# A fourth fixed expert in the MoE stage, and the routing tables moved into the output buffers

## The chip, the cores and the metric

One core of one Trainium2 chip runs the whole program in one launch. The metric is the device time of one execution in microseconds. Three runs of the kernel before took 2047.45, 2049.58 and 2053.73 us; their median is 2049.58 us.

## The reference, cut to what matters

The program is two layers of a decoder trunk on 1024 tokens of 1024 fp32 values. Layer 0 mixes with attention and state-space heads, layer 1 with a Conformer convolution. After each mixer comes the same hierarchical mixture of experts (MoE): 4 groups of 8 experts, the best group is chosen for a token, then the best 2 experts in that group, so that 2048 (token, expert) pairs fall on 32 experts in whatever way the router decides. Nothing may be dropped.

```python
g_sel = jnp.argmax(g_logits, axis=-1)
g_w = jnp.take_along_axis(jax.nn.softmax(g_logits, axis=-1), g_sel[:, None], axis=-1)[:, 0]
e_logits = jnp.take_along_axis(e_all, g_sel[:, None, None], axis=1)[:, 0]
top_v, top_i = lax.top_k(e_logits, 2)
gate = (g_w[:, None] * jax.nn.softmax(top_v, axis=-1)).reshape(-1)
eid = (g_sel[:, None] * 8 + top_i).reshape(-1)
...
gu = xb @ w_gate_up[e]                                  # 1024 x 1024 weights of expert e
y = (silu(gu[:, :512]) * gu[:, 512:]) @ w_down[e]       # 512 x 1024
...
x = x + sum over the token's two experts of gate * y
```

## The kernel before, in words

The program is one sequence of stages: mixer of layer 0, MoE of layer 0, Conformer of layer 1, MoE of layer 1. `moe(k, layer)` is the function that the change touches; it runs twice.

**Routing.** PE makes the router's logits, DVE picks the choices `M` (two 0/1 masks of 128 x 8 x 32), PE counts them (L1417, L1418), and DVE makes each pair's rank in its expert (`rank`) and, through one-hot matmuls, a table of which token stands at which rank of which expert (`tabT`). From it come `hidx` (the rows to gather for an expert) and `yidx` (where its output rows go).

**Order and capacity.** Experts 0 to FIXED-1 are worked on first, whatever their counts; that allows their weights to be fetched before the counts are known. Each fixed expert has room for 96 tokens, which is three blocks of TB = 32. The other experts are sorted by count (`nth`, then `place`, then `order`): the FULL = 2 largest have room for 128 tokens, the next LARGE = 13 for 96, the rest for 64. `place_of` sets at which place in the sequence each rank of the sort stands, so that long and short experts alternate. There are 84 blocks in all. An expert's tokens beyond its capacity are *overflow*: `count_overflow` and `place_overflow` compute how many extra passes of 128 rows are needed (`n_over`), `index_overflow` says where each overflowing pair stands.

**The stream of weights.** SP issues all weight loads on one queue: 4 MB of gate-up and 2 MB of down per expert. Gate-up has four buffers (the fourth is the residual `x_res`, which has been parked in DRAM by then), down has three. Down buffer 2 holds the routing tables until they are done with. Experts 0 to 2 come in early; the fourth buffer's first load (L1207 waits for `order_ready`) and the third down load (behind `over_ready`) come when the sort and the overflow tables are finished. From there on the load of expert q waits for PE to be through with the buffer's last user.

**One block.** PE multiplies 32 tokens by gate-up (64 matmuls, L1458), ACT takes silu of one half (L1285), DVE the product (L1627) and a transpose (L1631), PE multiplies by down (32 matmuls, L1473) one block later, ACT copies the result to one of YB = 6 output buffers (L1279, `y_evacuate`), and POOL scatters it to `y_rows` in DRAM by an indirect DMA (L1346). POOL also gathers the rows of an expert by an indirect DMA (L1339), PE turns them (L1440), DVE evacuates them (`xT_evacuate`, L1620).

**Behind the last block.** Each engine reads `n_over` and enters its loop `over` only where that is above 0 (`turns_over`). In such a pass POOL first scatters the overflow table to DRAM (`table`: 16 indirect DMAs), SP waits for them all, then loads 128 slot numbers, the 4 MB and 2 MB of the overflowing expert's weights; POOL gathers the rows, PE turns them and does 64 matmuls of 128 x 128 and 8 of 128 x 512, ACT and DVE the rest, and POOL scatters 128 rows; SP waits for that (`o_stored`). Then, in layer 1, SP loads `y_rows` back (L1250), DVE adds them to `x` (L1712), and SP writes the output.

The output buffers `rows_in_out` hold three gather buffers `xg` (3 x 1024 columns) and six output buffers `y` (6 x 256).

Of the kernel before, what the change touches and what calls it, by code (L numbers as in the profile page):

```python
# [19 lines left out]
AX = mybir.AxisListType  # L20

P = 128
D = 1024
T = 1024
NT = T // P
# [15 lines left out]
NE = NG * EG  # L41
# [7 lines left out]
TB = 32  # L49
FIXED, FULL, LARGE = 3, 2, 13  # L50


XB, YB = 3, 6
TURNS, LAST_FULL = 12, 17
AHEAD = 3
# [977 lines left out]
def moe(k, layer):  # L1033
# [3 lines left out]
    PAD = 1 << 16  # L1037
# [9 lines left out]
    with ExitStack() as ctx:  # L1047
# [18 lines left out]
        def early(shape):  # L1066
            n = math.prod(shape[1:])
            flat = tables[:, used[0]:used[0] + n]
            used[0] += n
            assert used[0] <= KF * D, used  # L1070
            return shaped(flat, shape)

        def part_of(flat, at0, shape):
            return shaped(flat[:, at0:at0 + math.prod(shape[1:])], shape)
# [13 lines left out]
        h = rows_in_out[:, 0:2 * D].rearrange("p (b n) -> p b n", b=2)  # L1088
        y_spare = rows_in_out[:, 4 * D:]
        L = k.logits  # L1090
# [12 lines left out]
        ge, go = sb("ge", [P, NT, NG]), sb("go", [P, NT, NG])  # L1103
        E, W = early([P, NT, NE]), early([P, NT, NE])
        M = early([P, 2, NT, NE])
        M_flat = M[:, :, :, :].rearrange("p j i e -> p (j i) e")
        Msel = early([P, 2, NT, NE])
        in_Msel = Msel[:, :, :, :].rearrange("p j i e -> p (j i e)")
        scan_mask = part_of(in_Msel, 0, [P, NE, NT + 1])
        in_group, met = part_of(in_Msel, 288, [P, NT, EG]), part_of(in_Msel, 352, [P, NT, EG])  # L1110
        rank_sel, fold_sorted = part_of(in_Msel, 416, [P, 2 * NT]), part_of(in_Msel, 432, [P, NE])
        empty, place_col = part_of(in_Msel, 464, [P, NE]), part_of(in_Msel, 496, [P, 1])
        Msel_flat = Msel[:, :, :, :].rearrange("p j i e -> p (j i) e")
        both = early([P, NE, NT + 1])
        top = [sb("top1_", [P, NT]), sb("top2_", [P, NT])]
        ex, den = sb("ex", [P, NT]), sb("m_den", [P, NT])
        pre = early([P, NE, NT + 1])
        rank = early([P, NE, NT])
        key = early([P, NE])
# [12 lines left out]
        order_f = early([P, NE])  # L1132
        cap_e, excess = early([P, NE]), early([P, NE])
        extra, incl, shift, oe = behind[3], behind[4], behind[5], sb("oe", [P, MAX_OVER])
# [18 lines left out]
        fold_ready, chosen, v_ready = sem("fold_ready"), sem("chosen"), sem("m_v_ready")  # L1153
        over_ready, padded, table_made = sem("over_ready"), sem("padded"), k.dma_sems[layer]["table_made"]
        dve_link, pool_link = sem("m_dve_link"), sem("m_pool_link")
# [40 lines left out]
        def _(sp):  # L1196
# [8 lines left out]
            sp.wait_ge(h_ready, NT - SQUARED_EARLY)  # L1205
            sp.wait_ge(x_parked, 16 * (SQUARED_EARLY + 1))
            sp.wait_ge(order_ready, 1)  # L1207
            down = 2
            for q in range(FIXED, NE + 1):
                if q < NE:  # L1210
                    e = sp.value_load(order[0:1, q:q + 1], min_val=0, max_val=NE - 1)
                    if q > FIXED:
                        sp.wait_ge(gu_done, last_of[gu_user[q]] + 1)
                    load_gate_up(sp, e, gu_of[q])
                if q == FIXED:
                    sp.wait_ge(over_ready, 1)
                else:
                    sp.wait_ge(d_done, last_of[q - 4] + 1)
                load_down(sp, down, (q - 1) % 3)
                down = e  # L1220
# [36 lines left out]
        def _(act):  # L1257
# [17 lines left out]
            def y_evacuate(n):  # L1275
                act.wait_ge(d_done, n + 1)
                if n >= YB:
                    act.wait_ge(stored[n % YB], 16 * (n // YB))
                act.activation(y[:, n % YB, :], ps[:, Y + n % 2, 0:D // 4], ACT.Copy).then_inc(y_ready, 1)  # L1279
# [20 lines left out]
        def _(pool):  # L1300
# [37 lines left out]
            def gather(q):  # L1338
                pool.indirect_dma_start(out=xg[:, q % XB, :], out_offset=None, in_=k.hbuf,  # L1339
                                        in_offset=bass.IndirectOffsetOnAxis(ap=hidx[:, q:q + 1], axis=0),  # L1340
                                        bounds_check=last_h, oob_is_err=False).then_inc(gathered[q % XB], 16)
# [18 lines left out]
            for q in range(XB):  # L1360
                gather(q)
            pool.wait_ge(h_index, 2)
            pool.wait_ge(turned, 1)
            pool.wait_ge(gathered[0], 16)
            gather(XB)
            pool.wait_ge(y_index, 1)
            for q in range(NE):
# [140 lines left out]
        def _(dve):  # L1508
# [98 lines left out]
            ts(fold_sorted[:], eid[:], place_col[:, 0:1], None, ALU.is_equal).then_inc(fold_ready, 1)  # L1607
            link(tt(cmp[:], eid[:, :].unsqueeze(2).to_broadcast([P, NE, NE]), place[:, :].unsqueeze(1).to_broadcast([P, NE, NE]), ALU.is_equal))
            dve.wait_ge(spread, 2)
            row_index(ps[:, TOTALS, FIXED:NE], FIXED, NE)  # L1610
            link(tt(cmp[:], cmp[:], eid[:, :].unsqueeze(1).to_broadcast([P, NE, NE]), ALU.mult))
            dve.wait_ge(spread, 3)
# [5 lines left out]
            def xT_evacuate(p, tokens, out):  # L1618
                for half in range(2):
                    tt(xT[:, p, 4 * half:4 * half + 4, 0:tokens], ps[:, TRN + half, :].rearrange("p (k t) -> p k t", k=4)[:, :, 0:tokens],  # L1620
                       g_exp[:, 4 * half:4 * half + 4].unsqueeze(2).to_broadcast([P, 4, tokens]), ALU.mult).then_inc(out, 1)
# [10 lines left out]

            def sort_weights():
                link(dve.tensor_reduce(order_f[:], cmp[:], AX.X, ALU.add))
                dve.tensor_copy(order[:], order_f[:]).then_inc(order_ready, 1)
# [34 lines left out]
            def index_overflow():  # L1670
                link(tt(E[:], rank[:].rearrange("p e i -> p i e"), in_tiles(cap_e[:], NE), ALU.is_lt))
                link(tt(W[:], rank[:].rearrange("p e i -> p i e"), in_tiles(shift[:], NE), ALU.add))
                link(stt(out=W[:], in0=E[:], scalar=float(PAD), in1=W[:], op0=ALU.mult, op1=ALU.add))
                for j in range(2):
                    link(tt(Msel[:, j, :, :], M[:, j, :, :], W[:], ALU.mult))
                link(dve.tensor_reduce(posf[:], Msel_flat, AX.X, ALU.add))
                link(dve.tensor_copy(pos[:], posf[:]))
                dve.sem_inc(over_ready, 1)

            sort_weights()  # L1680
            dve.wait_ge(turned, 1)
            xT_evacuate(0, CAP[0], xT_ready)
            count_overflow()
            place_overflow()
            for n in range(NB):
                q, tl = blocks_of[n]
                hidden(n)
                if tl == 0 and q + 1 < NE:
                    dve.wait_ge(turned, q + 2)
                    xT_evacuate((q + 1) % 2, CAP[q + 1], xT_ready)  # L1690
                if n == 0:
                    index_overflow()
                if n == 3:
                    weigh_choices()
# [606 lines left out]
```

## Time and profile before

| | |
|---|---|
| median of three runs | 2049.58 us |
| the profiled execution | 2048.27 us, span 2046.5 us |
| PE, PE weight loads, DVE, ACT, POOL busy | 91%, 56%, 43%, 21%, 20% of the span |
| mixer of layer 0 with its routing | 0 to 546 us |
| experts of layer 0 | 546 to 1045 us |
| Conformer of layer 1 with its routing | 1045 to 1507 us |
| experts of layer 1 | 1507 to 2005 us |
| sum of the outputs | 2005 to 2046.5 us |

The span runs from the first to the last instruction. The stages were told apart by the lines that run in them. Times in the views are us from the span's start, and a wait is put down to whoever ended it.

### The profile page before, as it was taken

The page shows a single profiled execution, that of the slowest core. Times are in us where ns is not written, and L with a number is a line of the kernel's source. Part 1 is how long each engine was busy: PE and PEld are TensorE (multiplying, and loading weights), DVE is VectorE, ACT ScalarE, POOL GpSimd, SP SyncE. Part 2 cuts the span into 40 slices and gives each one's busy share as a digit, 9 for nine tenths or more (in the row PEclk, how much of TensorE's full clock was granted, in tenths as well). Part 3 has the DMA queues.
Part 4 walks back from the last instruction along what each step waited for, and adds up shares of the span by engine and source line. Part 5 has one row for each costly group of instructions (what it writes and reads, how often), then busy time and mean ns, then how long its engine had stood idle before and what let it go on. Part 6 is the DMA issues. An engine that isn't in the chain of part 4 may idle for free. (4 is left out here: it accounts for less than half of the span.)

```text
span 2046.5 us, 46991 instructions
## 1 busy us (share of the span) xinstructions
PE 1863.8 (91%) x20566; PEld 1148.5 (56%) x20566; DVE 886.1 (43%) x1980; ACT 427.4 (21%) x965; POOL 406.0 (20%) x524
## 2 busy tenths in 40 slices
PE   7999999999699999889969999799879999998892
PEld 5677766666466665656545444345546666655561
DVE  3666666664711111111135999893371121111114
ACT  2433332344011111101023122234401111100110
POOL 2211111012122222222122111120122222222110
PEclk9999999999699999999979999899979999999996
DMA  9200000044699999999887456413589999999996
GB/s 324 80 11 1 11 10 10 0 185 182 259 426 425 427 424 425 426 427 426 369 321 211 86 113 134 108 32 134 217 327 418 425 425 429 425 426 426 425 388 275
DMA packets 94256, 541.95 MB, mean 265 GB/s; under 512 B 23366, under 2 KB 46970, under 8 KB 76392
## 3 DMA queue, kind: packets, MB, share of 16 engines
q1 hardware_dynamic: 68376, 479.13, 57.2%
q0 software_dynamic: 23040, 51.43, 9.0%
q10 hardware_dynamic: 2640, 8.44, 1.0%
q8 instruction: 160, 2.62, 0.5%
q14 instruction: 40, 0.33, 0.1%
HBM read 504.29 MB, written 43.03 MB: 267 GB/s over the span
## 5 line engine op out<-in xcount | busy, mean ns | idle before, releaser
L1627 DVE TENSOR_TENSOR acts<-acts,ps 128x128 f32<-128x128 f32 x168 | 66.3, 395 | 692.0 <-ACT acts L1285 691.6
L1346 POOL DMA_INDIRECT y_rows<-rows_in_out,yidx x168 | 166.6, 992 | 761.5 <-ACT rows_in_out L1279 751.6
L1458 PE MATMUL ps<-wgu,xT 128*32 128x256 f32 x5376 | 306.6, 380 | 0.0
L1473 PE MATMUL ps<-wd,acts 128*32 128x256 f32 x3520 | 215.4, 386 | 26.2 <-issue 23.1
L1458 PEld LDWEIGHTS ps<-wgu,xT 128*32 128x32 f32 x5376 | 176.7, 110 | 109.9 <-issue 5.3
L1285 ACT ACTIVATE acts<-ps 128x128 f32<-128x128 f32 x168 | 46.6, 277 | 632.9 <-PE ps L1458 632.9
L1473 PEld LDWEIGHTS ps<-wd,acts 128*32 128x32 f32 x3520 | 120.1, 111 | 101.9 <-issue 29.9
L1458 PE MATMUL ps<-x_res,xT 128*32 128x256 f32 x2816 | 165.4, 388 | 0.0
L1458 PE MATMUL ps<-early_gu,xT 128*32 128x256 f32 x2560 | 149.7, 387 | 4.1 <-DVE xT L1620 4.1
L2223 DVE SCALAR_TENSOR_TENSOR conv<-dd,par,conv 128x256 f32<-128x256 f32 (+1 forms) x255 | 131.4, 589 | 0.2
L1458 PEld LDWEIGHTS ps<-x_res,xT 128*32 128x32 f32 x2816 | 96.0, 113 | 60.9 <-issue 7.8
L1279 ACT ACTIVATE rows_in_out<-ps 128x256 f32<-128x256 f32 x168 | 64.5, 384 | 292.9 <-PE ps L1473 292.9
L1473 PE MATMUL ps<-early_wd,acts 128*32 128x256 f32 x1856 | 113.5, 385 | 13.1 <-issue 13.1
L864 PEld LDWEIGHTS ps<-m_hT,early_gu 128*128 128x128 f32 x1024 | 116.1, 192 | 4.6 <-issue 3.3
L1458 PEld LDWEIGHTS ps<-early_gu,xT 128*32 128x32 f32 x2560 | 84.0, 112 | 60.5 <-issue 6.7
L864 PE MATMUL ps<-m_hT,early_gu 128*128 128x128 f32 x1024 | 116.9, 275 | 0.7 <-DMA early_gu<-in_w_in 0.7
L1850 PE MATMUL ps<-c_hT,early_wd 128*128 128x512 f32 x256 | 112.7, 593 | 3.4 <-ACT sig L2011 3.2
L1886 PE MATMUL ps<-w_pw,c_hT 128*128 128x512 f32 x256 | 112.4, 593 | 1.5 <-ACT c_hT L2028 1.5
L1858 PE MATMUL ps<-c_hT,early_wd 128*128 128x512 f32 x256 | 112.5, 592 | 0.0
L1620 DVE TENSOR_TENSOR xT<-ps,g_exp 128x384 f32<-128x384 f32 (+2 forms) x128 | 58.9, 502 | 100.2 <-PE ps L1440 100.2
L1473 PEld LDWEIGHTS ps<-early_wd,acts 128*32 128x32 f32 x1856 | 63.1, 111 | 52.8 <-issue 16.7
L918 PE MATMUL ps<-w_out_sb,m_yT 128*128 128x512 f32 x192 | 86.3, 602 | 0.0
(354 smaller groups left out, 2204.5 us busy)
## 6 DMA issues: line engine op xcount, KB each, us to landing
wgu<-in_moe_w_gate_up SPq DMA_DIRECT2D x32, 4096.0 KB, 30.7
wd<-in_moe_w_down SPq DMA_DIRECT2D x42, 2048.0 KB, 29.6
early_gu<-in_moe_w_gate_up SPq DMA_DIRECT2D x18, 4096.0 KB, 29.9
x_res<-in_moe_w_gate_up SPq DMA_DIRECT2D x14, 4096.0 KB, 25.7
early_wd<-in_moe_w_down SPq DMA_DIRECT2D x22, 2048.0 KB, 24.7
early_wd<-in_conv_w_pw SPq DMA_DIRECT2D x22, 512.0 KB, 5.4
conv<-prod POOLq DMA_DIRECT2D x20, 512.0 KB, 4.5
x_res<-x_park SPq DMA_DIRECT2D x2, 4096.0 KB, 31.4
```

Of the source, the lines that this page charges most:

```text
L864: mm = pe.matmul(ps[:, bank, (t % 4) * P:(t % 4 + 1) * P], w_x[:, j, t * P:(t + 1) * P], hT[:, j, :], start=(j == 0), stop=(j == KD - 1))
L918: mm = pe.matmul(ps[:, bank, :], attn_T[p][:, j, :] if j < 4 else yT[:, j, :], w_out[:, j, 512 * half:512 * half + 512], start=(j == 0), s ...
L1279: act.activation(y[:, n % YB, :], ps[:, Y + n % 2, 0:D // 4], ACT.Copy).then_inc(y_ready, 1)
L1346: pool.indirect_dma_start(out=y_quarters, out_offset=bass.IndirectOffsetOnAxis(ap=yidx[:, tl, q:q + 1], axis=0), in_=y[:, n % YB, :], in_o ...
L1458: mm = pe.matmul(ps[TB * g:TB * g + TB, GU + n % 2, 0:2 * P].rearrange("p (a f) -> p a f", a=2), xT[:, q % 2, j, TB * tl:TB * tl + TB], wg ...
L1473: mm = pe.matmul(ps[TB * g:TB * g + TB, Y + n % 2, 0:D // 4], hhT[:, n % 2, TB * j:TB * j + TB], wd[q % 3][:, j, D // 4 * g:D // 4 * g + D ...
L1620: tt(xT[:, p, 4 * half:4 * half + 4, 0:tokens], ps[:, TRN + half, :].rearrange("p (k t) -> p k t", k=4)[:, :, 0:tokens], g_exp[:, 4 * half ...
L1627: tt(hh[:, n % 2, :].rearrange("q (k f) -> q k f", k=KF), by_k(sg[:, n % 2, :]), by_k(ps[:, GU + n % 2, P:2 * P]), ALU.mult).then_inc(hh_r ...
L1850: mm = pe.matmul(ps[:, GATE, :], wg[:, p, j, :], hT[:, j, HALF * h:HALF * h + HALF], start=(j == 0), stop=(j == KD - 1))
L1858: mm = pe.matmul(ps[:, LIN + n % 2, :], wa[:, p, j, :], hT[:, j, HALF * h:HALF * h + HALF], start=(j == 0), stop=(j == KD - 1))
L1886: mm = pe.matmul(ps[:, BACK + half, :], yT[:, j, :], w_pw2[:, j, 512 * half:512 * half + 512], start=(j == 0), stop=(j == CT - 1))
L2223: ins = dve.scalar_tensor_tensor(out=out[s], in0=dd[:, s, q + k0:q + k1], scalar=par[:, c, 2 * q - 1 + s:2 * q + s], in1=out[s] if r else ...
```

## The change: what it does

FIXED goes from 3 to 4 and LARGE from 13 to 12, LAST_FULL from 17 to 16; the blocks stay 84. SP loads expert 3's gate-up into the fourth buffer once the first gathered rows have landed, and expert 2's down weights once a new semaphore `tables_free` says that the tables in down buffer 2 are done with; it waits for `order_ready` only then. For this, the choices `M`, the ranks and the temporaries of `index_overflow` move from down buffer 2 into output buffers, and ACT's first copy into an output buffer waits for `over_ready`. The three steps that sort the weights' order, two comparisons of 128 x 1024 and a sum, move behind the evacuation of the first expert's tokens. POOL issues the fourth gather before it waits for the later experts' indices.

```diff
-FIXED, FULL, LARGE = 3, 2, 13
+FIXED, FULL, LARGE = 4, 2, 12
-TURNS, LAST_FULL = 12, 17
+TURNS, LAST_FULL = 12, 16
...
-        E, W = early([P, NT, NE]), early([P, NT, NE])
-        M = early([P, 2, NT, NE])
+        E, W = early([P, NT, NE]), part_of(y_spare, 0, [P, NT, NE])
+        M = part_of(y_first, 0, [P, 2, NT, NE])
+        in_cap, picked = part_of(y_first, 768, [P, NT, NE]), part_of(y_spare, 256, [P, NT, NE])
-        rank = early([P, NE, NT])
+        rank = part_of(y_first, 512, [P, NE, NT])
...
             sp.wait_ge(x_parked, 16 * (SQUARED_EARLY + 1))
+            sp.wait_ge(gathered[0], 16)
+            load_gate_up(sp, 3, 3)
+            sp.wait_ge(tables_free, 1)
+            load_down(sp, 2, 2)
             sp.wait_ge(order_ready, 1)
-            down = 2
+            down = 3
             for q in range(FIXED, NE + 1):
                 if q < NE:
                     e = sp.value_load(order[0:1, q:q + 1], min_val=0, max_val=NE - 1)
-                    if q > FIXED:
-                        sp.wait_ge(gu_done, last_of[gu_user[q]] + 1)
+                    sp.wait_ge(gu_done, last_of[gu_user[q]] + 1)
                     load_gate_up(sp, e, gu_of[q])
-                if q == FIXED:
-                    sp.wait_ge(over_ready, 1)
-                else:
-                    sp.wait_ge(d_done, last_of[q - 4] + 1)
+                sp.wait_ge(d_done, last_of[q - 4] + 1)
                 load_down(sp, down, (q - 1) % 3)
                 down = e
...
             def y_evacuate(n):
                 act.wait_ge(d_done, n + 1)
+                if n == 0:
+                    act.wait_ge(over_ready, 1)
...
-            pool.wait_ge(h_index, 2)
             pool.wait_ge(turned, 1)
             pool.wait_ge(gathered[0], 16)
             gather(XB)
+            pool.wait_ge(h_index, 2)
             pool.wait_ge(y_index, 1)
...
-            link(tt(cmp[:], eid[:, :].unsqueeze(2)..., place[:, :].unsqueeze(1)..., ALU.is_equal))
             dve.wait_ge(spread, 2)
             row_index(ps[:, TOTALS, FIXED:NE], FIXED, NE)
-            link(tt(cmp[:], cmp[:], eid[:, :].unsqueeze(1)..., ALU.mult))
...
             def sort_weights():
+                link(tt(cmp[:], eid[:, :].unsqueeze(2)..., place[:, :].unsqueeze(1)..., ALU.is_equal))
+                link(tt(cmp[:], cmp[:], eid[:, :].unsqueeze(1)..., ALU.mult))
                 link(dve.tensor_reduce(order_f[:], cmp[:], AX.X, ALU.add))
                 dve.tensor_copy(order[:], order_f[:]).then_inc(order_ready, 1)
...
                 for j in range(2):
-                    link(tt(Msel[:, j, :, :], M[:, j, :, :], W[:], ALU.mult))
-                link(dve.tensor_reduce(posf[:], Msel_flat, AX.X, ALU.add))
+                    link(tt(picked[:], M[:, j, :, :], W[:], ALU.mult))
+                    link(dve.tensor_reduce(posf[:, NT * j:NT * j + NT], picked[:], AX.X, ALU.add))
...
-            sort_weights()
             dve.wait_ge(turned, 1)
             xT_evacuate(0, CAP[0], xT_ready)
+            sort_weights()
             count_overflow()
             place_overflow()
+            dve.sem_inc(tables_free, 1)
             for n in range(NB):
                 q, tl = blocks_of[n]
                 hidden(n)
```

## Rows read from the trace of the kernel before

**Rows 1.** Busy time by stretch: length, each engine's busy us, PE clock, DMA share, GB/s.
```profile
1772.00:1945.00 173.00, 154.55 (x2597) 98.31 (x2600) 28.18 (x74) 17.16 (x52) 36.99 (x37) 0.96 1.01 425
...
2004.00:2046.50 42.50, 2.57 (x48) 1.30 (x40) 20.52 (x17) 0.77 (x2) 1.96 (x2) 0.57 0.77 303
```
**Rows 2.** Chain that ended last, from 1935 to 1962: start, us, what.
```profile
1938.76 2.00 issue
1940.76 2.65 PE ps L1473 x32
1943.41 4.42 PE ps L1458 x64
...
1959.36 1.73 PE ps L1473 x32
```
**Rows 3.** DMA issues from 1921.5 to 1922: KB, us to landing.
```profile
wd<-in_moe_w_down SPq DMA_DIRECT2D x1, 2048.0 KB, 36.1
```
**Rows 4.** DMA queues from 1497.9 to 1505.5, layer 1's first three gathers: packets, MB; issue to landing.
```profile
q0 software_dynamic: 429, 0.90, 42.1%
...
rows_in_out<-h_rows,hidx POOLq DMA_INDIRECT x3, 4.2
```
**Rows 5.** The same from 1505.5 to 1510: the fourth gather, the fourth gate-up.
```profile
q0 software_dynamic: 147, 0.26, 19.9%
...
x_res<-in_moe_w_gate_up SPq DMA_DIRECT2D x1, 4096.0 KB, 13.3
rows_in_out<-h_rows,hidx POOLq DMA_INDIRECT x1, 3.4
```
**Rows 6.** Instructions in order of time, 1455 to 1545, layer 1's first expert.
```profile
1499.81 1.01 POOL L1339 DMA_INDIRECT rows_in_out<-h_rows,hidx  x1 [0.30 <-issue]
...
1500.78 1.22 DVE L1608 TENSOR_TENSOR wd<-early_gu,wd 128x1024 f32<-128x1024 f32 x1
...
1501.12 1.73 POOL L1339 DMA_INDIRECT rows_in_out<-h_rows,hidx  x1 [0.31 <-issue]
...
1503.14 1.95 PE L1440 MATMUL ps<-ident,rows_in_out 128*128 128x128 f32 x8
...
1506.12 1.01 DVE L1620 TENSOR_TENSOR xT<-ps,g_exp 128x384 f32<-128x384 f32 x2
...
1507.05 0.35 SPq L1180 DMA_DIRECT2D x_res<-in_moe_w_gate_up  x1
...
1507.19 5.89 PE L1458 MATMUL ps<-early_gu,xT 128*32 128x256 f32 x64 [2.10 <-DVE xT L1620]
...
1513.81 0.39 DVE L1627 TENSOR_TENSOR acts<-acts,ps 128x128 f32<-128x128 f32 x1
...
1519.05 0.33 SPq L1183 DMA_DIRECT2D wd<-in_moe_w_down  x1
...
1523.09 0.34 SPq L1180 DMA_DIRECT2D early_gu<-in_moe_w_gate_up  x1
```
**Rows 7.** Chain that ended last, from 2003 to 2013: the last scatter and what follows.
```profile
2007.30 3.45 DMA y_rows<-rows_in_out,yidx
...
2011.72 0.33 SPq L1250
```
**Rows 8.** Groups of instructions in the mixer of layer 0: count, busy us, mean ns.
```profile
L864 PE MATMUL ps<-m_hT,early_gu 128*128 128x128 f32 x64 | 7.3, 275 | 0.0
...
L918 PE MATMUL ps<-w_out_sb,ycat 128*128 128x512 f32 x8 | 3.6, 592 | 0.0
...
L608 ACT ACTIVATE s<-ps 128x512 f32<-128x512 f32 x4 | 2.2, 594 | 0.5 <-PE ps L906 0.5
```
**Rows 9.** DMA issues of other stretches: 1465.6 to 1466.1, and 1521.9 to 1531.
```profile
token_slot<-pad SPq DMA_DIRECT2D x1, 16.0 KB, 3.8
...
early_gu<-in_moe_w_gate_up SPq DMA_DIRECT2D x1, 4096.0 KB, 15.8
...
rows_in_out<-h_rows,hidx POOLq DMA_INDIRECT x1, 15.5
```

More of the change, by code:

```diff
@@ L1088, in moe @@
         h = rows_in_out[:, 0:2 * D].rearrange("p (b n) -> p b n", b=2)
-        y_spare = rows_in_out[:, 4 * D:]
+        y_first, y_spare = rows_in_out[:, XB * D:4 * D], rows_in_out[:, 4 * D:]
         L = k.logits
@@ L1103, in moe @@
         ge, go = sb("ge", [P, NT, NG]), sb("go", [P, NT, NG])
-        E, W = early([P, NT, NE]), early([P, NT, NE])
-        M = early([P, 2, NT, NE])
+        E, W = early([P, NT, NE]), part_of(y_spare, 0, [P, NT, NE])
+        M = part_of(y_first, 0, [P, 2, NT, NE])
+        in_cap, picked = part_of(y_first, 768, [P, NT, NE]), part_of(y_spare, 256, [P, NT, NE])
         M_flat = M[:, :, :, :].rearrange("p j i e -> p (j i) e")
-        Msel = early([P, 2, NT, NE])
-        in_Msel = Msel[:, :, :, :].rearrange("p j i e -> p (j i e)")
+        in_Msel = early([P, 512])
         scan_mask = part_of(in_Msel, 0, [P, NE, NT + 1])
@@ L1112, in moe @@
         empty, place_col = part_of(in_Msel, 464, [P, NE]), part_of(in_Msel, 496, [P, 1])
-        Msel_flat = Msel[:, :, :, :].rearrange("p j i e -> p (j i) e")
         both = early([P, NE, NT + 1])
@@ L1132, in moe @@
         order_f = early([P, NE])
-        cap_e, excess = early([P, NE]), early([P, NE])
+        cap_e, excess = sb("cap_e", [P, NE]), early([P, NE])
         extra, incl, shift, oe = behind[3], behind[4], behind[5], sb("oe", [P, MAX_OVER])
@@ L1153, in moe @@
         fold_ready, chosen, v_ready = sem("fold_ready"), sem("chosen"), sem("m_v_ready")
-        over_ready, padded, table_made = sem("over_ready"), sem("padded"), k.dma_sems[layer]["table_made"]
+        over_ready, tables_free, padded, table_made = sem("over_ready"), sem("tables_free"), sem("padded"), k.dma_sems[layer]["table_made"]
         dve_link, pool_link = sem("m_dve_link"), sem("m_pool_link")
@@ L1607, in _ @@
             ts(fold_sorted[:], eid[:], place_col[:, 0:1], None, ALU.is_equal).then_inc(fold_ready, 1)
-            link(tt(cmp[:], eid[:, :].unsqueeze(2).to_broadcast([P, NE, NE]), place[:, :].unsqueeze(1).to_broadcast([P, NE, NE]), ALU.is_equal))
             dve.wait_ge(spread, 2)
             row_index(ps[:, TOTALS, FIXED:NE], FIXED, NE)
-            link(tt(cmp[:], cmp[:], eid[:, :].unsqueeze(1).to_broadcast([P, NE, NE]), ALU.mult))
             dve.wait_ge(spread, 3)
@@ L1633, in sort_weights @@
             def sort_weights():
+                link(tt(cmp[:], eid[:, :].unsqueeze(2).to_broadcast([P, NE, NE]), place[:, :].unsqueeze(1).to_broadcast([P, NE, NE]), ALU.is_equal))
+                link(tt(cmp[:], cmp[:], eid[:, :].unsqueeze(1).to_broadcast([P, NE, NE]), ALU.mult))
                 link(dve.tensor_reduce(order_f[:], cmp[:], AX.X, ALU.add))
@@ L1670, in index_overflow @@
             def index_overflow():
-                link(tt(E[:], rank[:].rearrange("p e i -> p i e"), in_tiles(cap_e[:], NE), ALU.is_lt))
+                link(tt(in_cap[:], rank[:].rearrange("p e i -> p i e"), in_tiles(cap_e[:], NE), ALU.is_lt))
                 link(tt(W[:], rank[:].rearrange("p e i -> p i e"), in_tiles(shift[:], NE), ALU.add))
-                link(stt(out=W[:], in0=E[:], scalar=float(PAD), in1=W[:], op0=ALU.mult, op1=ALU.add))
+                link(stt(out=W[:], in0=in_cap[:], scalar=float(PAD), in1=W[:], op0=ALU.mult, op1=ALU.add))
                 for j in range(2):
-                    link(tt(Msel[:, j, :, :], M[:, j, :, :], W[:], ALU.mult))
-                link(dve.tensor_reduce(posf[:], Msel_flat, AX.X, ALU.add))
+                    link(tt(picked[:], M[:, j, :, :], W[:], ALU.mult))
+                    link(dve.tensor_reduce(posf[:, NT * j:NT * j + NT], picked[:], AX.X, ALU.add))
                 link(dve.tensor_copy(pos[:], posf[:]))
                 dve.sem_inc(over_ready, 1)
-            sort_weights()
             dve.wait_ge(turned, 1)
             xT_evacuate(0, CAP[0], xT_ready)
+            sort_weights()
             count_overflow()
             place_overflow()
+            dve.sem_inc(tables_free, 1)
             for n in range(NB):
```

## The prediction

> **What bounds the kernel now.** Read the busy time by stretch first. In the second half of layer 1's experts the 16 DMA engines are full, at 425 GB/s, while PE works for 154.6 of 173 us [rows 1]: the weights come at the rate at which DMA brings them, and PE follows closely. The chain of waits shows where: PE stops before the first down product of a three-block expert, the last time for 2.0 us until 1940.76, and that product and the next gate-up, at a clock that has just fallen, take 2.65 and 4.42 us instead of 1.73 and about 3.5 [rows 2], some 1.9 us more. Then the DMA issues: the down weights of the next expert land at 1921.7 + 36.1 = 1957.8 [rows 3], and PE asks for them at 1959.36 [rows 2], so DMA is 1.6 us ahead there and PE sets the rest. Behind the last block nothing is slow: the last scatter lands 3.45 us after 2007.30, and SP loads the outputs back at 2011.72 [rows 7]. No engine enters its loop `over`, since nothing overflows.
>
> **Whether that stays so is the first question.** Only experts with a capacity of their rank in the sort are safe; a fixed one has 96 whatever its count. So I counted. The reference's routing, followed through with its inputs, gives experts 0 to 3 73, 70, 74 and 76 pairs in layer 0, and 76, 60, 85 and 119 in layer 1. The trace bears this out: layer 1's first three gathers moved 0.90 MB [rows 4], which is 220 rows of 4 KB against 76 + 60 + 85 = 221, and the fourth moved 0.26 MB [rows 5], 63 rows; by the sort before, the fourth place holds rank 10, which has 62. In the kernel before, expert 3 of layer 1 is the second largest and gets 128 places. Fixed, it gets 96: 23 pairs overflow, `n_over` is 1 in layer 1, and every engine goes once through `over`. In layer 0 nothing overflows, and the other experts fit in both layers.
>
> **Front of each MoE stage.** The tokens of expert 0 are turned at 1503.14 + 1.95 = 1505.09, but DVE takes them only at 1506.12, behind the sort [rows 6]; it will come 1.0 us earlier. The sort then stands between there and the first product: three operations of 1.2 us (the two comparisons and the sum; one row stands for them) and a copy of 0.2, 3.9 us with their gaps. So the product at 1513.81 [rows 6] comes 2.9 us later; PE meanwhile has two gate-ups and a turn, and loses 0.2 us at most in layer 1, about 1 in layer 0, where the first gate-up was quicker. `index_overflow` grows by 0.2 us (two sums of 256 for one of 512). ACT's new wait for `over_ready` holds the second silu's successor, and behind it the first scatter on POOL; both end before PE wants the freed PSUM bank, so I cost it at nothing, and at 1 us per layer if that cover fails. The fourth gather on POOL waits for `turned` anyway, and the wait that moves behind it is over by then: nothing.
>
> SP issues gate-up 3 when the first rows have landed: gathers take 4.2 us [rows 4] and the first was issued before 1499.81 [rows 6], so at about 1503 instead of 1507.05, and down 2 at about 1517 instead of 1519.05. The load after these waits in both kernels for PE to be through with expert 0, 1523.09 [rows 6]; the stream behind it gains only what queue it no longer finds there, 0 to 1 us. The second gather, issued at 1499.81, has all but landed by then; the third and fourth share DMA with gate-up 3, and PE wants them 20 us and more later.
>
> One three-block expert moves from near the end to the front. The last wait then falls on the expert of 1957.8 rather than that of 1940.76, 1.6 us better, plus the stream's 0 to 1, plus 1.9 if the clock doesn't fall once more. That is 0.5 to 4 us a layer. I take 1.5 for each of the two layers, **3 us less**; bounds 8 less to 3 more (the front's losses without the gain).
>
> **The pass through `over`, layer 1.** No row of before shows it, so each piece is bounded by its nearest rows. It lies bare: SP loads `y_rows` only when it has ended.
> - POOL's table: 16 indirect DMAs behind the last scatter, which starts at 2007.30. One takes 1.0 us of POOL and 0.3 until the next [rows 6]: 16 x 1.3 = 20.8 from about 2008.3; the last starts at 2027.8 and lands 3.45 later, 2031.3. Below: no gaps, 4.8 less. Above: 1.73 + 0.31, as a gather's longest row [rows 6], 12 more; each waiting for the one before to land, 16 x 3.45, 34 more.
> - SP: slot load and register reads, 1.2 us by the 0.97 between landing and next issue [rows 7] and one more issue of 0.3. Gate-up of expert 3 once more, alone on the queue: 13.3 us [rows 5]. Down is 2.1 MB behind it at the 425 GB/s of a full stream [rows 1], 4.9. Together 19.4, so 2050.7. Below: gate-up at that rate too, 9.9, 3.4 less.
> - Beside this: slots 3.8 [rows 9], indices and POOL's start 1.4, the gather. Alone it lands in 3.4 [rows 5], beside a load in 15.5 [rows 9]. That one moved some 55 rows and this one moves 23, so I take 6.5. Turning takes 2 and evacuating 1.3 us: about 2047, hidden behind the weights. At 15.5 it would end 4 us behind them.
> - PE: 64 matmuls of 128 x 128, 7.3 us at the full clock [rows 8]. PE has stood idle for 40 us, and the clock of such a stretch is granted at 0.57 [rows 1], mostly the 1.2 GHz level; layer 1's first gate-up took 5.89 [rows 6], 2.3 over a later one. I take 9.6: 2060.3. Above: half clock throughout, 14.6.
> - silu, product and two copies of 128 x 512 at 0.6, down 3.6 [rows 8], 0.6 for six semaphores: 6.6, so 2066.9. Half clock adds 3.6.
> - Scatter: POOL's start 0.75, landing 3.45, SP 0.8: outputs are loaded at 2071.9 instead of 2011.72, **60 us later**. All that follows is the same.
>
> The Trainium skill (DMA: Bandwidth & Descriptors, section Anatomy of one DMA — SWDGE (gpsimd) path) has about 2.0 us a transfer plus bytes over 436 GB/s; as an estimate 6.3 MB in one piece would then take 16.4 us for my 18.2, and the total be 1.8 us less. The rows decide here, since the 13.3 is this load on this queue. The same page of the Trainium skill, section Queues, rings and completion order, says that each DMA engine goes round its queues packet by packet, so that a small gather need not stand behind a load; the gather of 15.5 beside a load of 15.8 doesn't look like it, and by that row without scaling the total is 4 us more.
>
> **Sum.** The profiled execution, 2048.27, is 1.3 under the median. 2048.3 - 3 + 60.2 + 1.3 = 2106.8; I say **2107**.
>
> **Rivals.**
> 1. *The pass is never entered* (not slower). It decides on one thing: whether expert 3 holds 96 or fewer in layer 1. Then only the front and the order act, 2049.6 - 3 = 2046.6. For it: the profile shows counts only as sums and ranks, none of expert 3 by itself. Against it: both numbers of rows fit the counts. 4%.
> 2. *The table is dear.* If the queue of indirect DMAs takes one at a time, 34 us more: 2141. For it: landings of 3.45 are longer than issues of 1.3. Against it: three gathers were issued within 4 us of each other, not one per landing [rows 6]. 8%.
> 3. *The front costs instead of gaining*: DVE's later product starves PE at the start of both stages, and DMA's queue runs dry behind PE; 3 us more in each, with the pass 2116. For it: layer 0's PE is already late by my sum. Against it: two gate-ups cover the sort. 10%.
> Forecast: 78%, with its own spread from 2092 to 2132.
>
> **How the numbers follow.** Low end: table and stream at their lower bounds, PE at full clock, the front at its best: 2107 - 4.8 - 3.4 - 2.3 - 5 = 2092. High end: the table's middle bound and half of the others: 2107 + 12 + 4 + 5 + 4 = 2132. Rival 3 is inside, rivals 1 and 2 are out. A measurement tells a change from none at about 0.3%, 6 us. Without the pass that is faster once in four and else the same: faster 0.01, same 0.04, slower 0.95.
>
> **What would show it.** In the changed profile: 16 indirect DMAs that write `token_slot` behind the last scatter, one more gate-up load by SP near the end, 64 and 8 matmuls under new lines, and the sum of outputs some 60 us behind the last block, in layer 1 alone; at the front the first evacuation about 1 us earlier and the first product 3 us later. If no `token_slot` is written, the forecast is wrong altogether; if POOL's table takes 50 us, only its price.

## The result and the profile after

The changed kernel takes **2132.4 us** (median of four runs, 2130.56 to 2134.67), the kernel before 2050.6 beside it: ratio 1.040, 95% interval 1.0387 to 1.0413. It is slower for the reason forecast, 25 us more than forecast and 0.4 us above the range.

The busy time of layer 1's end, by stretch, answers to [rows 1]: length, then busy us of PE, PE's weight loads, DVE, ACT and POOL, the granted clock, the share of DMA, GB/s. The stretches are the table, the load of the weights, the gate-up, the down, the scatter, and the sum of the outputs.

```profile
2004.00:2031.50 27.50, 4.06 (x76) 2.21 (x68) 0.71 (x2) 1.05 (x3) 17.66 (x18) 0.62 0.04 10
2031.50:2050.50 19.00, 1.97 (x8) 1.57 (x8) 1.05 (x4) 0.00 (x0) 1.04 (x1) 0.50 0.82 336
2050.50:2081.40 30.90, 30.13 (x128) 29.94 (x128) 0.55 (x1) 0.05 (x1) 0.00 (x0) 0.93 0.00 1
2081.40:2091.90 10.50, 8.52 (x16) 3.51 (x16) 0.69 (x1) 1.17 (x3) 0.00 (x0) 0.84 0.00 0
2091.90:2096.10 4.20, 0.00 (x0) 0.00 (x0) 0.00 (x0) 0.47 (x1) 1.00 (x1) 0.96 0.07 23
2096.10:2130.60 34.50, 0.00 (x0) 0.00 (x0) 20.17 (x16) 0.00 (x0) 0.00 (x0) 0.50 0.92 365
```

Apart from the gather and its turn, which run beside the load of the weights, one engine or DMA works at a time until the outputs are summed: the pass is a chain. The two PE stretches stand out, 30.13 and 8.52 us where the prediction had 9.6 and 3.6. The chain of waits (start, us, what) names its pieces and answers to [rows 7]:

```profile
2010.08 0.98 POOL token_slot L1352
...
2029.37 2.15 DMA token_slot<-slot_ids,pos
2031.76 1.97 DMA over_slot<-token_slot
...
2034.92 12.79 DMA rows_in_out<-h_rows,over_ih
2047.76 1.98 PE ps L1441 x8
2049.76 1.30 DVE xT L1619 x2
2051.19 30.14 PE ps L1495 x128
2081.35 0.60 ACT wd L1293
2081.98 0.70 DVE wd L1706
2082.73 8.53 PE ps L1502 x16
...
2093.17 2.60 DMA y_rows<-wd,over_slot
```

Sixteen writes of `token_slot`, 1.29 us apart, the slots, the gather, the turn, then two stretches of PE, and the scatter. The output rows are asked for at 2096.05, in the kernel before at 2011.72 [rows 7]. The DMA issues of the same pass (KB, us to landing) answer to [rows 5, 9]:

```profile
wgu<-in_moe_w_gate_up SPq DMA_DIRECT2D x1, 4096.0 KB, 12.6
wd<-in_moe_w_down SPq DMA_DIRECT2D x1, 2048.0 KB, 17.0
over_slot<-token_slot SPq DMA_DIRECT2D x1, 0.5 KB, 2.0
rows_in_out<-h_rows,over_ih POOLq DMA_INDIRECT x1, 12.8
```

The down weights, issued at 2033.49, land at 2050.5; the gather, issued at 2034.92, lands at 2047.7 and with the turn and the evacuation ends 0.6 us behind them. The groups of PE and of its weight loads (busy us, mean ns) answer to [rows 8]:

```profile
L1495 PE MATMUL ps<-xT,wgu 128*128 128x128 f32 x128 | 30.1, 403 | 1.5 <-DVE xT L1619 1.5
L1502 PE MATMUL ps<-wd 128*128 128x512 f32 x16 | 8.5, 694 | 1.4 <-DVE wd L1706 1.4
L1441 PE MATMUL ps<-ident,rows_in_out 128*128 128x128 f32 x8 | 2.0, 428 | 39.7 <-DMA rows_in_out<-h_rows,over_ih 39.7
```
```profile
L1495 PEld LDWEIGHTS ps<-xT,wgu 128*128 128x128 f32 x128 | 29.9, 329 | 1.9 <-DMA wd<-in_moe_w_down 1.9
L1502 PEld LDWEIGHTS ps<-wd 128*128 128x128 f32 x16 | 3.5, 227 | 5.8 <-issue 4.2 <-DVE wd L1706 1.6
```

The code has 64 products (calls of the matmul) at L1495 and 8 at L1502; the trace has 128 and 16 records. The eight transposes at L1441 are eight records. And the gate-up's weight loads are busy for 29.9 of its 30.1 us, at 329 ns each.

The front of layer 1 answers to [rows 6], in order of time:

```profile
1503.58 0.33 SPq L1179 DMA_DIRECT2D x_res<-in_moe_w_gate_up  x1
...
1506.12 1.02 DVE L1619 TENSOR_TENSOR xT<-ps,g_exp 128x384 f32<-128x384 f32 x2 [0.82 <-PE ps L1441]
...
1507.20 6.06 PE L1459 MATMUL ps<-early_gu,xT 128*32 128x256 f32 x64 [1.11 <-DVE xT L1619]
...
1517.73 0.33 SPq L1182 DMA_DIRECT2D wd<-in_moe_w_down  x1
1517.79 0.38 DVE L1626 TENSOR_TENSOR acts<-acts,ps 128x128 f32<-128x128 f32 x1
...
1518.57 1.93 PE L1474 MATMUL ps<-early_wd,acts 128*32 128x256 f32 x32 [0.70 <-DVE acts L1630]
...
1524.19 0.34 SPq L1179 DMA_DIRECT2D early_gu<-in_moe_w_gate_up  x1
```

The routing ahead of it ended 1.07 us later in this execution, so that gate-up, which begins at 1507.20 and before at 1507.19, begins 1.06 us earlier relative to it (18.27 us behind the ranks' product, 19.33 before). In layer 1 the ranks' product is counted here and below from the second of its two records, in layer 0 from the first, which starts 0.64 us before it. Gate-up 3 and down 2 go out at 1503.58 and 1517.73, as forecast; the first product comes at 1517.79. The chain near the end of layer 1's experts answers to [rows 2]:

```profile
1954.88 0.32 DVE acts L1630
1955.20 3.76 issue
1958.96 3.40 PE ps L1474 x32
1962.36 3.66 PE ps L1459 x62
```

The last wait has moved on by one expert, from 1940.76 to 1958.96, and behind it the clock falls again: the granted clock is 0.55 while the down product takes 3.40 us; in the kernel before it was 0.70 during the 2.65 us of [rows 2].

### The profile page after: what moved, and what is told of

The parts are those of the page before. It is cut to its first block and busy times, and to the rows that moved or that the text cites. A ratio compares the mean times of both kernels' runs of the same rounds, so it can differ in the third digit from the quotient of the medians.

```text
span 2130.6 us, 47348 instructions
## 1 busy us (share of the span) xinstructions
PE 1908.5 (90%) x20718; PEld 1181.9 (55%) x20718; DVE 890.1 (42%) x1987; ACT 428.7 (20%) x968; POOL 422.0 (20%) x542
## 5 line engine op out<-in xcount | busy, mean ns | idle before, releaser
L1459 PE MATMUL ps<-early_gu,xT 128*32 128x256 f32 x3456 | 205.0, 390 | 2.2 <-DVE xT L1619 2.2
L1459 PEld LDWEIGHTS ps<-early_gu,xT 128*32 128x32 f32 x3456 | 115.6, 113 | 81.3 <-issue 12.0
L864 PEld LDWEIGHTS ps<-m_hT,early_gu 128*128 128x128 f32 x1024 | 116.1, 192 | 4.7 <-issue 3.3
L864 PE MATMUL ps<-m_hT,early_gu 128*128 128x128 f32 x1024 | 116.9, 275 | 0.7 <-DMA early_gu<-in_w_in 0.7
L1459 PE MATMUL ps<-x_res,xT 128*32 128x256 f32 x1920 | 109.6, 380 | 0.0
L1441 PE MATMUL ps<-ident,rows_in_out 128*128 128x128 f32 x520 | 73.6, 286 | 39.7 <-DMA rows_in_out<-h_rows,over_ih 39.7
L1441 PEld LDWEIGHTS ps<-ident,rows_in_out 128*128 128x128 f32 x520 | 58.1, 145 | 65.7 <-DMA rows_in_out<-h_rows,over_ih 40.2
```

The source lines that it names most:

```text
L864: mm = pe.matmul(ps[:, bank, (t % 4) * P:(t % 4 + 1) * P], w_x[:, j, t * P:(t + 1) * P], hT[:, j, :], start=(j == 0), stop=(j == KD - 1))
L1441: mm = pe.transpose(columns, xg[:, buf, j * P:(j + 1) * P], ident[:])
L1459: mm = pe.matmul(ps[TB * g:TB * g + TB, GU + n % 2, 0:2 * P].rearrange("p (a f) -> p a f", a=2), xT[:, q % 2, j, TB * tl:TB * tl + TB], wg ...
```

## The experiments

**e1: the pass alone taken away.**

```diff
-link(dve.tensor_copy(n_over[:], incl[:, NE - 1:NE]))
+link(dve.memset(n_over[:], 0))
```


> The changed kernel with n_over set to 0, so that the pass through over is skipped (the 23 pairs beyond expert 3's capacity in layer 1 are left out). Theory: the pass is the whole loss, and all the rest of the change comes to nothing that can be measured; SP loads the outputs some 84 us earlier, at about 2012 us, and the time is 2047 to 2051 us, a ratio to the kernel before of 0.998 to 1.001. Rival, the front or the stream of weights also costs: above 2055 us. Rival, my term of 3 us less holds: 2045 to 2048.

Measured: 2051.2 us over 11 runs, ratio to before 1.0008 (0.9999 to 1.0017). The pass is the whole loss: 2132.4 - 2051.2 = 81.2 us. And the rest of the change, which was to gain 3 us, gains nothing.

**e2: no overflow, because expert 3 gets room for 128.**

```diff
-FIXED, FULL, LARGE = 4, 2, 12
+FIXED, FULL, LARGE = 4, 2, 11
-by_place = [3 * TB] * FIXED + [0] * n
+by_place = [3 * TB] * (FIXED - 1) + [4 * TB] + [0] * n
```


> The changed kernel with 128 places for expert 3 instead of 96 and one three-block expert fewer behind it (LARGE 11), 84 blocks as before; nothing overflows. Theory: as without the pass, 2046 to 2052 us, with the one longer expert at the front now giving DMA 5 us more to get ahead, so that PE's waits late in the stage come to less than the 19 us of layer 1 now. Rival, that a fixed fourth expert costs by itself: above 2055 us.

Measured: 2053.7 us over 11 runs, ratio 1.0021 (1.0012 to 1.003). The loss is gone but for 0.2%, 1.7 us above the range that I had expected: the overflow was the cause, and four fixed experts with enough room gain nothing either. In its trace layer 0 takes 522.9 us from the ranks' product to the last scatter (518.3 in the changed kernel), with one wait more for weights, 3.9 us at 1031.8.

**e3: the pass's gate-up weights read in neighbouring columns.**

```diff
-wgu[OVER][:, i, :].rearrange("p (a f k) -> p a k f", a=2, k=KF)[:, f // KF, f % KF, :]
+wgu[OVER][:, i, :].rearrange("p (a k f) -> p a k f", a=2, k=KF)[:, f // KF, f % KF, :]
```


> The changed kernel with the pass's 64 products reading 128 neighbouring columns of gate-up as PE's weights instead of every fourth (other columns, same number). If the stride makes a weight load dear, the weight loads fall from 329 ns to about 192 and the 128 matmul instructions from 30.1 us to 14.6 to 17 us, and the time is 2115 to 2119 us. If the clock or the number of instructions alone makes it dear, 30 us stay and the time is 2130 to 2134 us.

Measured: 2117.9 us, 14.4 less. In the traces the gate-up is 14.2 us shorter and the down 1.4, and the pass begins 1.1 us later. The group of weight loads of this line in e3, to be held against that of the changed kernel above:

```profile
L1495 PEld LDWEIGHTS ps<-xT,wgu 128*128 128x128 f32 x128 | 15.8, 207 | 1.9 <-DMA wd<-in_moe_w_down 1.9
```

The same 128 records: 207 ns each instead of 329, and 15.8 us in all instead of 29.9. With every fourth column taken, a weight load is 122 ns longer, and the records come 110 ns further apart (235 and 124 ns). What is left, 124 ns a record, is near the prediction's price (7.3 us for 64 records, 114 ns [rows 8]); the rest of the miss is the number of records.

These means hide the clock. The same loads while the granted clock was 0.50 and then while it was 1.00, first in the changed kernel (2051.2 to 2054, 2055.5 to 2081), then in e3 (2052.5 to 2055, 2056.5 to 2068):

```profile
L1495 PEld LDWEIGHTS ps<-xT,wgu 128*128 128x128 f32 x13 | 3.1, 327 | 1.9 <-DMA wd<-in_moe_w_down 1.9
L1495 PEld LDWEIGHTS ps<-xT,wgu 128*128 128x128 f32 x110 | 25.8, 329 | 0.0
```
```profile
L1495 PEld LDWEIGHTS ps<-xT,wgu 128*128 128x128 f32 x12 | 2.6, 329 | 1.9 <-DMA wd<-in_moe_w_down 1.9
L1495 PEld LDWEIGHTS ps<-xT,wgu 128*128 128x128 f32 x105 | 11.8, 192 | 0.0
```

The strided load takes the same time at either level, and its records come 233 ns apart at both. At stride one they come 213 ns apart at the half clock and 112 at the full one. So the stride costs 20 ns a record at the half clock and 121 at the full clock, where most of the records fall.

**e11: half of the products.**

```diff
-for i in range(KD):
+for i in range(KD // 2):
```


> The changed kernel with half of the gate-up products in the pass (the other half of the input columns is left out of the sum for the 23 pairs). Theory A: the pass's gate-up is bound by its own weight loads, 234 ns a record and two records a product: 64 records in 15.1 us in place of 128 in 30.1, and 2132 - 15 = 2117. Rival: something else paces it (an arrival of weights in pieces, the clock): the stretch shrinks by clearly less than half, and the time by 5 to 10 us.

Measured: 2115.4 us, 17 less. The group of PE:

```profile
L1495 PE MATMUL ps<-xT,wgu 128*128 128x128 f32 x64 | 15.2, 409 | 1.5 <-DVE xT L1619 1.5
L1502 PE MATMUL ps<-wd 128*128 128x512 f32 x16 | 7.1, 599 | 1.4 <-DVE wd L1706 1.4
```

32 calls are 64 records and 15.2 us: theory A. The down was 1.4 us quicker, the other part of the 17, since the half clock that fell into it in the changed kernel (granted 0.57 from 2082.7 to 2086) didn't here (1.00).

**e4: the pass's weights loaded ahead of its table.** SP's two loads go out as soon as the buffers are free; the wait for the table and the read of the slots stand behind them.

> The changed kernel with SP loading the overflowing expert's weights before it waits for the table, instead of behind it. If the weights were the last to arrive in the pass, the gather now has the queue to itself (about 4 us instead of 12.8) and PE starts its products 8 to 10 us sooner: 2122 to 2125 us. If the gather's own path sets it, no more than 3 us: 2129 to 2133 us.

Measured: 2122.5 us, 9.9 less. The loads leave at 2013.34, the weights are long there, and the first product is at 2042.88 in place of 2051.19. What ends last now is the table with the gather behind it: the table alone keeps the pass waiting until 2032.97, when the slots are asked for.

**e5: e1 with the sort put back ahead of the first evacuation.**

```diff
-xT_evacuate(0, CAP[0], xT_ready)
-sort_weights()
+sort_weights()
+dve.wait_ge(turned, 1)
+xT_evacuate(0, CAP[0], xT_ready)
```


> The changed kernel without a turn through the pass (23 pairs of layer 1 are left out of the output, as in e1) and with the sort of the weights put back ahead of the first evacuation, where the kernel before had it. Theory A: the first gate-up that starts 1.06 us earlier is worth its 1 us per layer only while PE doesn't wait for weights later, and it does in both layers, so the move is worth 0 to 1 us in all: 2051 to 2052, the same as e1 (2051.2) within what can be told. Rival: the move is worth its full 1.06 us in both layers, and other parts of the change ate it: 2053.3, and the stretch from the ranks to the first gate-up back at 19.3 us.

Measured: 2052.5 us over 11 runs, ratio to the kernel before 1.0008 (0.9999 to 1.0017), the same as e1's. The delay came out larger than the rival said, since both comparisons now stand there too: gate-up begins 21.2 us behind the ranks' product, 2.9 later than in e1. In layer 0 the last scatter nevertheless stands 518.95 us behind that product (e1: 518.79), in layer 1 523.3 (e1: 520.6). So layer 0 takes up the whole 3 us; in layer 1 the one trace shows it lost, and the medians, 1.3 us apart with as wide an uncertainty, neither confirm nor exclude it.

**e6: the kernel before once more.**

> The kernel before, unchanged, for a second trace. In its first trace the Conformer of layer 1 and all ahead of it took 412.9 us up to the router of layer 1's expert stage, in the changed kernel and its variants 414.9 to 416.6. Theory A: this is chance (which stretches run at the half clock): a second trace of the kernel before gives another value, some 413 to 417. Rival: the changed kernel slows that stretch: 412.9 again within 0.5.

Measured: 2051.7 us, span 2050.0. From the first Conformer matmul to layer 1's router 415.6 us, against 412.9 in its first trace, 415.0 in the changed kernel, 416.6 in e1 and 413.1 in e9. Theory A: two traces of one kernel differ by 2.7 us there, and the 2 to 4 us by which that stretch is longer in the traces of after and e1 than in the first trace of before need not be an effect of the change.

**e7: the kernel before, made to overflow.**

```diff
-FIXED, FULL, LARGE = 3, 2, 13
+FIXED, FULL, LARGE = 3, 1, 14
```


> The kernel before with one place of 128 fewer and one of 96 more in its sorted experts, so that 5 pairs of layer 0 and 23 of layer 1 overflow, and nothing else of the change. One block of 32 tokens fewer in each layer, about 6 us each. Theory A: the price of the pass is its own, 81 us a layer as between e1 and the changed kernel, whatever stands around it: 2050 - 12 + 162 = 2200. Rival: in layer 0 the next Conformer's loads and rows hide part of it, 30 to 50 us: 2150 to 2170. Second rival: the pass is dear only by what the changed kernel does to it: two times 57: 2152.

Measured: 2211.6 us, 161 more than before: two passes at some 81. In layer 0, from the last scatter to the Conformer's first matmul, 91.5 us in place of 7.0; in layer 1, from the last scatter to the loads of the sums, 86.1 in place of 4.4. The price is the pass's own, in either layer and without the change; nothing of layer 1's Conformer hides it. The 12 us that I took off for two fewer blocks were not there: both expert stages lasted as before but for 4 us in layer 0. Where weights set the pace, a block less is not 6 us less.

**e8: a second turn of the pass, on an empty table.**

```diff
-link(dve.tensor_copy(n_over[:], incl[:, NE - 1:NE]))
+link(ts(n_over[:], incl[:, NE - 1:NE], 2.0, None, ALU.mult))
```


> The changed kernel with twice the number of turns: layer 1 goes through the pass a second time, on an empty table (nothing is gathered, nothing lands). Theory A: a turn without its table costs what the trace of the changed kernel shows from the read of the slots (2031.76) to the loads of the sums (2096.05), 64.3 us: 2197. Rival: part of the pass is the first entry into code that has not run, and a second turn costs clearly less, 45 to 55 us: 2177 to 2187.

Measured: 2196.1 us, 63.7 more (theory A: 64.3). The gate-up takes the same in the second turn as in the first, 30.13 us. The second turn:

```profile
2115.50 30.13 PE L1495 MATMUL ps<-xT,wgu 128*128 128x128 f32 x128 [1.46 <-DVE xT L1619]
2147.04 8.83 PE L1502 MATMUL ps<-wd 128*128 128x512 f32 x16 [1.41 <-DVE wd L1706]
```

From the read of the slots on, the first turn takes 64.5 us in this trace and the second 63.8: no more than 0.7 us of that is a first entry. The table ahead of it, some 23 us, is made only once, so that nothing is shown of it.

**e9: e3 and e4 in one, complete.** The down weights are loaded as rows `(k p)` so that they match the neighbouring columns of gate-up.

> The changed kernel with a pass that reads its gate-up weights in neighbouring columns (the down weights are loaded in the matching order, so that nothing of the computation is left out) and loads its weights ahead of its table: e3 and e4 in one. Theory A: the two savings are of different terms (14.4 of the products, 10 of the loads) and add: 2132 - 24 = 2108. Rival: with the weights there early the chain runs over the table, the slots and the gather, and some of the 10 is lost to the down weights, which are now read in pieces of 4 KB: 2113 to 2118.

Measured: 2107.2 us. 25.2 less, where e3 and e4 saved 14.4 and 9.9: the savings add; theory A.

**e10: the table made while the experts run.**

```diff
...
 scatter(n)
+if n == 20:
+    pool.wait_ge(over_ready, 1)
+    pool.wait_ge(padded, 16)
+if 20 <= n < 20 + 2 * NT:
+    over_slots(n - 20)
...
```


> The kernel of e9 with its table made while the experts run: GpSimd issues one of the 16 indirect writes behind each of 16 scatters from the 21st on, whether the pass is entered or not. Theory A: behind the last scatter no table stands any more, the weights are asked for at once (about 2011.5) and are there 17.5 us later (2029), and from there to the loads of the sums the chain of the changed kernel needs 45.6 us less 14.2 for the stride and 1.4 for the down: 30, so that these are asked for at 2059 in place of 2096.05: 2095. Rival: 16 writes of 1 us on GpSimd between scatters delay scatters and gathers, and the experts' stage grows by some us in both layers: 2100 to 2115. In both cases still slower than before, by over 40 us.

Measured: 2104.5 us over four runs, ratio 1.0269 (1.0252 to 1.0286). By its number the rival, by its mechanism neither: the two expert stages together are as long as in the changed kernel (first gate-up to last scatter 502.1 and 499.6 us; there 499.3 and 501.6), so the 16 writes cost 1 us there at most. The 9 us that theory A lacks are in the DMA issues of the pass, SP's queue being the new bound:

```profile
wgu<-in_moe_w_gate_up SPq DMA_DIRECT2D x1, 4096.0 KB, 12.1
wd<-in_moe_w_down SPq DMA_DIRECT2D x1, 2048.0 KB, 16.6
over_slot<-token_slot SPq DMA_DIRECT2D x1, 0.5 KB, 16.3
rows_in_out<-h_rows,over_ih POOLq DMA_INDIRECT x1, 3.3
```

I had kept the order of e4, weights first. With no table left to cover it, the read of 512 bytes waited for 6.3 MB that had been issued ahead of it on the same queue.

**e12: e10 with the slots asked for ahead of the weights.**

> The kernel of e10 (2104.5) with the read of the slots asked for ahead of the two weight loads. In e10 its 0.5 KB stood behind 6.3 MB on SP's queue and took 16.3 us. Theory A: the slots are there at about 2015, the gather lands while the weights come, and the gate-up begins when the weights are there, about 2030 in place of 2037.65: 2104.5 - 7.5 = 2097. Rival: the gather's 92 KB beside the weight load take 12.8 to 15.5 us, as beside a load in the kernel before and in the changed one, and it is the gather that ends last: turn at 2031, gate-up at 2035: 2102.

Measured: 2096.3 us, theory A. The same view:

```profile
wgu<-in_moe_w_gate_up SPq DMA_DIRECT2D x1, 4096.0 KB, 12.6
wd<-in_moe_w_down SPq DMA_DIRECT2D x1, 2048.0 KB, 17.2
...
over_slot<-token_slot SPq DMA_DIRECT2D x1, 0.5 KB, 2.0
rows_in_out<-h_rows,over_ih POOLq DMA_INDIRECT x1, 11.4
```

The slots take 2.0 us instead of 16.3, the gather beside the weights 11.4 instead of 3.3, and it is the weights that end last (first product 2030.85). This is the cheapest version with the pass, 36 us under the changed kernel and still 46 us above the kernel before. No version was faster than the kernel before; the nearest one that computes everything is e2, 0.2% slower.

## Why the prediction was wrong

The cause, the rows of it and the sign were right: expert 3 overflows with 23 pairs in layer 1, each engine goes once through `over`, and nothing else costs more than a few us (e1, e2). Neither rival 1 nor rival 2 happened: `token_slot` is written, and the 16 writes stand 1.29 us apart. The size failed in two terms. In the profiled executions the forecast was 2105.5 and the trace shows 2132.3, 26.8 more: 22.6 in the pass and 4.5 ahead of it, less 0.2 behind. That the time came within 0.4 us of the range's top is luck: 12 us of that top stood for a dearer table, which didn't come, and nothing in it for a second record a product or for a stride. ("Half of the others" is not what was added there: 4, 5 and 4 are the whole bounds of the gather, the gate-up and the down, and the front's is left out.)

- *Table and weights.* From the last scatter to the landed weights 43.4 us were forecast and 41.7 came (2050.45 - 2008.79). Right, each piece within 1.5 us.
- *The gather.* 6.5 forecast, 12.8 came, and 11.4 in e12 beside the same load; without one 3.3 (e9, e10). Scaling the row of 15.5 [rows 9] by the number of rows was wrong: what makes it long is mostly the load beside it, and little its own size. It cost 0.6 us, since the weights came nearly as late. The Trainium skill (DMA: Bandwidth & Descriptors, section Queues, rings and completion order) says that each engine goes round its queues packet by packet, and gives no time for such a gather. What I drew from it, that a small gather need not stand behind a load, didn't come: 23 rows took 12.8 us beside the load and 3.3 without one.
- ***PE: "64 matmuls of 128 x 128, 7.3 us at the full clock", with the clock 9.6: the step that failed.*** It took 30.1. Two mistakes. First, the row of the price counts 64 records [rows 8], and I read them as 64 calls. The line behind it, L864, is 4 x 8 = 32 calls; a matmul in fp32 is two records. The text ahead of the prediction mixes the two already: its 64 and 32 matmuls of a block (L1458, L1473) are records of 32 and 16 calls, its 64 and 8 of the pass are calls. The same holds for the down, whose 8 records in [rows 8] are four calls: 3.6 forecast, 8.5 came. By the right count the price at stride one is 128 x 114 ns = 14.6, and e3 measures 15.9 with the clock in it. Second, the pass loads every fourth column of its buffer as weights, and no row of before has such a load; I set no bound for it. It costs 329 instead of 207 ns a load, 14.2 us in all (traces of e3 and the changed kernel). The clock, which I had added, is hardly in it: 233 ns a record at either level. The Trainium skill (SBUF — State Buffer, section Door 1: The DMA port swizzle) says that SBUF has lines of 16 bytes and that each access into a new line pays; four fp32 columns are such a line, so by it this load pays at every column, and e3 agrees, since the stride alone was changed. The same passage gives 4 fp32 as how far one can stride for free; for this load a stride of four was not free, 329 ns against 192 at the full clock, and the measurement decides. That the line of 16 bytes is the reason no run shows: no other stride was tried. The upper bound, 14.6, was half of what came. The right count at the half clock throughout, 29.2, would look like the 30.1 as well, but the granted clock was 0.93 there, and e3 rules it out.
- *The rest of the pass.* silu, product, copies and scatter: forecast 8.0 without the down, in the trace some 6.2 (2081.3 to 2096.05 less 8.5). Near enough.
- *"3 us less" from the front and the order: it was 1.5 more in the trace, and by e1's ratio, 1.0008, between 0.2 less and 3.5 more.* The steps happened (evacuation 1.07 us earlier and product 2.9 us later, both counted from the ranks' product, the two early loads, PE's waits of 0.7 and 0.46 us). What they were to bring is seen by stretch:

| stretch | before | e6 | after | e1 |
|---|---|---|---|---|
| layer 0: ranks to last scatter | 521.9 | 522.0 | 518.3 | 518.8 |
| last scatter to the Conformer | 7.0 | 7.4 | 8.4 | 8.4 |
| Conformer | 412.9 | 415.6 | 415.0 | 416.6 |
| router to ranks, layer 1 | 19.9 | 19.9 | 20.8 | 19.9 |
| layer 1: ranks to last scatter | 519.4 | 519.8 | 519.9 | 520.6 |

  Layer 0 gained 3.1 to 3.6 us in these two (0.8 to 4.3 over all traces of the changed order but e2, which lost 0.9), more than the 1.5 forecast. Part of it is given back at once: the last scatter of layer 0 now goes out together with the Conformer's last weight load (1044.79 and 1044.77) instead of 3.5 us behind it (1048.04 and 1044.58) and takes 6.0 us to land, 4.9 before, and everything waits for it (the second row of the table). Layer 1 gained nothing (519.4 and 519.8 before; 517.6 to 520.8 over the traces without e5). Its start must be taken out first: the ranks' product stands 1.07 us later in this trace. Counted from it, the down weights that decide land 469.9 us on in both kernels (1958.9, and the 1957.8 that I had taken over from [rows 3]), though gate-up 6 goes out 0.7 us later (1558.2, before 1556.5). So the stream is where I had put it, and counted so the last wait ends 1.5 us before PE came to that point in the kernel before, near my 1.6. But the clock falls behind this wait too, and the down product and the gate-up take 1.9 us more than there (3.40 us for 1.73 [rows 2], 3.66 for 3.45). Together that is 0.4 us lost, the table's 519.9 for 519.4. I had put the clock on the wrong side of the sum, as 1.9 more to gain if it doesn't fall once more. The 1959.36 of the kernel before has its fall behind it already, so that 1.6 is the gain without a new fall, and with one 0.3 is lost.
- *Rival 3* (PE late at the front, the stream behind it, 6 us) didn't happen: the waits of 0.7 and 0.46 us are there, but the weights that decide come no later. e5 adds that even 3 us more at the front are taken up by layer 0's wait for the weights; why layer 1 took less of them stays open.

## What to carry to other kernels

Before a duration of a trace prices new code, count what one record is: divide the row's count by the calls of its line. A capacity that was tied to a sorted rank and is now tied to a name must be held against that name's count in every layer; a fallback that "never runs" is serial and unpolished, here 81 us for 23 pairs, of which 36 could be had back by making its table early, reading its weights in neighbouring columns and asking for the small read ahead of the large one. Time won or lost ahead of a stream of weights need not show behind it: in layer 0 the stream took up all of 3 us (e5). A sum that moves a wait must move what stands behind it too, here a fall of the clock that cost 1.9 us at either place.

## What the runs showed of the hardware

- A stationary operand (PE's weights) read at a stride of four columns, with the moving side unchanged: a load of 128 x 128 fp32 took 327 to 329 ns at a granted clock of 0.50 and of 1.00 alike, and the matmul records came 233 ns apart. At stride one (e3) it took 329 ns and 213 at 0.50, 192 and 112 at 1.00.
- One fp32 matmul of these kernels leaves two records and a transpose one: 64 calls 128 records, 32 calls 64 (e11), 8 transposes 8.
- A read of 0.5 KB behind two weight loads on SP's queue: 16.3 us against 2.0 (e10, e12).
- DVE and POOL at once on the same inputs: in layer 1's routing the two operations below start together; in some traces (the changed kernel, e2, e3, e5, e7, e8, e12) they took 1.51 (DVE) and 1.05 us (POOL); in others, as in both of before and e1, about 0.61 and 1.40. First the changed kernel, then e1:

```profile
1486.72 1.05 POOL L1357 TENSOR_TENSOR acts<-rows_in_out,slot_next 128x512 f32<-128x512 f32 x1 [10.62 <-DVEq L1555]
1486.72 1.51 DVE L1556 TENSOR_TENSOR wd<-rows_in_out 128x256 f32<-128x256 f32 x1
```
```profile
1487.57 1.40 POOL L1357 TENSOR_TENSOR acts<-rows_in_out,slot_next 128x512 f32<-128x512 f32 x1 [10.58 <-DVEq L1555]
1487.57 0.61 DVE L1556 TENSOR_TENSOR wd<-rows_in_out 128x256 f32<-128x256 f32 x1
```

It looks as if one of the two holds the other up, and which one differs from execution to execution, with e7 in the kernel before too; when it is DVE, the ranks' product comes 0.9 us later, the 20.8 in the table above. That was not tried by itself.
